# Mixture-of-experts loop: down-projection sums in the gate's banks, an earlier routing plan and an earlier row load

## The reference

```
probs = softmax(ht @ router); vals, idx = top_k(probs, 2)
gates = weights of the two chosen experts, normalised to sum 1
for e in range(8):
    out += gates[:, e:e+1] * (silu(ht @ w_gate[e]) * (ht @ w_up[e])) @ w_down[e]
```

## Time and profile before

| | us |
|---|---|
| median of 3 runs | 1326.36 |
| lowest and highest of them | 1324.71, 1326.44 |
| the profiled execution | 1324.71 |
| its span, first to last instruction | 1322.5 |
| PE busy | 1273.0 |
| DVE busy | 929.1 |
| ACT busy | 820.6 |

### The profile page before, as it was taken

The page is one execution under the profiler, slowest core; times in us unless marked ns, Lnnn a source line. Parts: engine busy times, 40 slices in busy tenths (PEclk is TensorE's granted clock), DMA queues, the critical chain, the costliest instruction groups (busy, mean ns, idle before and its releaser), DMA issues.

```text
span 1322.5 us, 15853 instructions
## 1 busy us (share of the span) xinstructions
PE 1273.0 (96%) x6057; PEld 1034.8 (78%) x6057; DVE 929.1 (70%) x926; ACT 820.6 (62%) x905; POOL 40.8 (3%) x52
## 2 busy tenths in 40 slices
PE   7999999999999899999999999999899998999998
PEld 6888888778887688867886788778678876788886
DVE  4776455446759878899889988998877564645542
ACT  5645444336866677788778877886577565544431
POOL 4001000000000200000000000002010000000000
PEclk9999999999999999999999999999999999999999
DMA  9648654544227989999999999999774241555440
GB/s 324 237 149 271 208 183 168 180 147 133 97 96 294 387 342 372 382 391 396 401 392 389 415 405 380 393 408 394 275 254 160 96 160 64 191 190 191 166 152 32
DMA packets 89855, 339.45 MB, mean 257 GB/s; under 512 B 6267, under 2 KB 14160, under 8 KB 66128
## 3 DMA queue, kind: packets, MB, share of 16 engines
q1 hardware_dynamic: 86816, 328.64, 66.8%
q0 software_dynamic: 2816, 9.89, 2.2%
q10 hardware_dynamic: 160, 0.07, 0.0%
HBM read 332.02 MB, written 9.44 MB: 258 GB/s over the span
## 4 chain that ended last, share of the span: by engine, by line
PE 73%; DVE 10%; issue 6%; ACT 5%; DMA 5%; POOL 0%; SPq 0%; ACTq 0%; DVEq 0%
PE bank L1886 23%; PE bank L1888 22%; PE bank L1887 22%; DVE w_lo L375 7%; DMA raw_beside<-in_moe_w_down 2%; ACT w_hi L370 2%; DMA moe_slots_in<-h,row_to 1%; DMA raw<-in_moe_w_up 1%; PE bank L1998 1%; PE bank L2025 1%; PE bank L2241 1%; DMA raw<-in_conv_w_in 1%; POOL moe_slots_in L592 0%; DMA rows_in<-moe_slots_in 0%; DVE x L1178 0%
## 5 line engine op out<-in xcount | busy, mean ns | idle before, releaser
L375 DVE TENSOR_TENSOR w_lo<-raw,w_hi 128x2048 fp32r<-128x2048 f32 (+3 forms) x246 | 548.4, 2245 | 205.0 <-ACT w_hi L370 204.3
L370 ACT ACTIVATE w_hi<-raw 128x2048 fp32r<-128x2048 f32 (+3 forms) x246 | 460.4, 1882 | 219.6 <-PE bank L1888 200.4
L1886 PE MATMUL bank<-w_hi,xT_hi 128*128 128x512 f32 (+2 forms) x672 | 255.9, 381 | 4.1 <-DVE xT_lo L1150 1.8
L1888 PE MATMUL bank<-w_hi,xT_lo 128*128 128x512 f32 (+2 forms) x672 | 252.9, 376 | 0.0
L1887 PE MATMUL bank<-w_lo,xT_hi 128*128 128x512 f32 (+2 forms) x672 | 252.7, 376 | 0.0
L375 DVE TENSOR_TENSOR w_lo<-raw_beside,w_hi 128x2048 fp32r<-128x2048 f32 x64 | 145.3, 2287 | 14.1 <-ACT w_hi L370 13.7
L1886 PEld LDWEIGHTS bank<-w_hi,xT_hi 128*128 128x128 f32 x672 | 126.4, 188 | 28.4 <-issue 3.6
L370 ACT ACTIVATE w_hi<-raw_beside 128x2048 fp32r<-128x2048 f32 x64 | 122.1, 1919 | 40.3 <-PE bank L1888 26.6
L1888 PEld LDWEIGHTS bank<-w_hi,xT_lo 128*128 128x128 f32 x672 | 126.4, 188 | 22.9
L1887 PEld LDWEIGHTS bank<-w_lo,xT_hi 128*128 128x128 f32 x672 | 126.5, 188 | 21.7
L1886 PE MATMUL bank<-w_hi,gT_hi 128*128 128x512 f32 x320 | 127.7, 399 | 2.1 <-DVE w_lo L375 1.7
(11 more groups left out here) (428 smaller groups left out, 1614.5 us busy)
## 6 DMA issues: line engine op xcount, KB each, us to landing
raw<-in_moe_w_gate SPq DMA_DIRECT2D x48, 1024.0 KB, 6.2
raw<-in_moe_w_up SPq DMA_DIRECT2D x48, 1024.0 KB, 7.9
raw_beside<-in_moe_w_down SPq DMA_DIRECT2D x32, 1024.0 KB, 10.7
raw<-in_moe_w_down SPq DMA_DIRECT2D x32, 1024.0 KB, 11.1
raw<-in_w_gate_up SPq DMA_DIRECT2D x22, 1024.0 KB, 5.2
raw_beside<-in_moe_w_gate SPq DMA_DIRECT2D x16, 1024.0 KB, 5.8
raw_beside<-in_moe_w_up SPq DMA_DIRECT2D x16, 1024.0 KB, 7.1
raw<-in_ffn_w_gate SPq DMA_DIRECT2D x11, 1024.0 KB, 5.1
```

The source lines that it names most:

```text
L370: nc.scalar.activation(w_hi[:, slot, :n], raw_of(i, stream)[:, :n], ACT.Copy).then_inc(stream.high, 1)
L375: nc.vector.tensor_tensor(w_lo[:, slot, :n], raw_of(i, stream)[:, :n], w_hi[:, slot, :n].bitcast(F32), ALU.subtract).then_inc(stream.low, 1)
L1886: mm(dst, a_hi, b_hi, start=start, stop=False)
L1888: return mm(dst, a_lo, b_hi, start=False, stop=stop)
```

## The change

Five things change. The down product of heavy and light experts goes to banks 0 and 1. The next expert's rows are transposed into banks 4 and 5 (heavy) or 6 and 7 (light), and the second folds of a light expert go to banks 4 and 5. PE waits for `moe_y` within the gate, after quarters 2 and 3 of chunks 0 and 1, instead of ahead of up, and asks for both chunks at its start; in `expert_put` it waits ahead of the gate. ACT's wait for `moe_y` ahead of silu and a wait of PE in the light expert go. In position 0 `positions` moves from c = 4 to c = 0, `rows_of_choices` from c = 5 to c = 1, and `load_rows(1)` from behind chunk 20 to behind chunk 14.

```diff
-                        if c == (14 if p else 20) and p < E - 1:
+                        if c == 14 and p < E - 1:
                             load_rows(p + 1)
...
                 def silu(e, number, quarter):
-                    act.wait_ge(sem("moe_y"), 1 + e)
...
-                        ins = A_(M["y"][:, half * HALF:(half + 1) * HALF], bank[4 + half][:, :], ACT.Copy)
+                        ins = A_(M["y"][:, half * HALF:(half + 1) * HALF], bank[half][:, :], ACT.Copy)
...
-                        ins = V.tensor_tensor(M["y"][:LIGHT, cols], bank[4 + half][:LIGHT, :], y_low[:, cols], ALU.add)
+                        ins = V.tensor_tensor(M["y"][:LIGHT, cols], bank[half][:LIGHT, :], y_low[:, cols], ALU.add)
...
-                        if first and c == 4:
+                        if first and c == 0:
                             positions()
-                        if first and c == 5:
+                        if first and c == 1:
                             rows_of_choices()
...
-                def gate(e, product):
-                    for k in range(KD):
+                def gate(e, product, y_read):
+                    first_two = [(k, weights(W1, MOE0 + k, e)) for k in range(2)]
+                    for quarter in (2, 3):
+                        for k, (wh, wl) in first_two:
+                            product(quarter, k, wh, wl, quarter)
+                    pe.wait_ge(sem("moe_y"), y_read)
+                    for k, (wh, wl) in first_two:
+                        for quarter in (0, 1):
+                            ins = product(quarter, k, wh, wl, quarter)
+                        ins.then_inc(W1.used, 1)
+                    for k in range(2, KD):
...
-                    gate(e, light_product)
+                    gate(e, light_product, 1 + e)
                     pe.wait_ge(sem("moe_act_done"), QUARTERS * e)
-                    pe.wait_ge(sem("moe_y"), 1 + e)
...
-                    pe.wait_ge(sem("moe_silu_done"), gated(e, 1))
...
-                        ins = fold_quarter(e_up, 2 + quarter // 2, quarter)
+                        ins = fold_quarter(e_up, 4 + quarter // 2, quarter)
...
-                    turn_rows(bank[0], 0)
-                    turn_rows(bank[1], 1)
+                    turn_rows(bank[4], 0)
+                    turn_rows(bank[5], 1)
...
-                        wide(W1, MOE0 + GU_CHUNKS + c, e, eth, etl, 2 * c, (4, 5), c == 0, c == FE // 256 - 1, tokens=1)
+                        wide(W1, MOE0 + GU_CHUNKS + c, e, eth, etl, 2 * c, (0, 1), c == 0, c == FE // 256 - 1, tokens=1)
...
                 def expert_put(e, h, n, number, job, last):
-                    if not last:
-                        pe.wait_ge(sem("moe_y"), E + 2 * n)
+                    pe.wait_ge(sem("moe_y"), E + 2 * n)
...
-                    if last:
-                        pe.wait_ge(sem("moe_y"), E)
```

More of the change, by code:

```diff
@@ L935, in light @@
                         if c in (17, 18):
-                            rows_high(number + c - 17, c - 17, c - 17)
+                            rows_high(number + c - 17, 6 + c - 17, c - 17)
                     act.wait_ge(W1.used, MOE0 + EXPERT_CHUNKS + EXPERT_CHUNKS * e)
                     for half in range(2):
-                        ins = A_(y_low[:, half * HALF:(half + 1) * HALF], bank[4 + half][LIGHT:, :], ACT.Copy)
+                        ins = A_(y_low[:, half * HALF:(half + 1) * HALF], bank[half][LIGHT:, :], ACT.Copy)
                     ins.then_inc(sem("light_copied"), 1)
@@ L951, in expert @@
                             turn_high(number + 1, 1)
-                            rows_high(number + 2, 0, 0)
+                            rows_high(number + 2, 4, 0)
                         if c == 16:
-                            rows_high(number + 3, 1, 1)
+                            rows_high(number + 3, 5, 1)
                             turn_high(number + 4, 2)
@@ L1578, in light_product @@
                     dve.wait_ge(sem("light_in_psum"), up_turned(i, j))
-                    V.tensor_tensor(M["e_act"][:, j, :], bank[2 + j][:, :], M["e_act"][:, 2 + j, :], ALU.mult)\
+                    V.tensor_tensor(M["e_act"][:, j, :], bank[4 + j][:, :], M["e_act"][:, 2 + j, :], ALU.mult)\
                         .then_inc(sem("moe_act_done"), 1)
@@ L1599, in light @@
                         if c in (17, 18):
-                            rows_low(n_high + c - 17, c - 17, c - 17)
+                            rows_low(n_high + c - 17, 6 + c - 17, c - 17)
                     dve.wait_ge(sem("light_copied"), y_copied(i))
@@ L1623, in expert @@
                             turn_low(n_high + 1, 1)
-                            rows_low(n_high + 2, 0, 0)
+                            rows_low(n_high + 2, 4, 0)
                         if c == 16:
-                            rows_low(n_high + 3, 1, 1)
+                            rows_low(n_high + 3, 5, 1)
                             turn_low(n_high + 4, 2)
@@ L2318, in light @@
                     pe.wait_ge(sem("moe_rows_loaded"), 16 + 16 * e)
-                    turn_rows(bank[0], 0)
-                    turn_rows(bank[1], 1)
+                    turn_rows(bank[6], 0)
+                    turn_rows(bank[7], 1)
                     for c in range(FE // 256):
@@ L2327, in light @@
                                 cols = slice(k * D + half * HALF, k * D + (half + 1) * HALF)
-                                ins = both(bank[4 + half][:, :], eth[:, 2 * c + k, :], wh[:, cols], wl[:, cols],
+                                ins = both(bank[half][:, :], eth[:, 2 * c + k, :], wh[:, cols], wl[:, cols],
                                            c == 0 and k == 0, c == FE // 256 - 1 and k == 1)
@@ L2333, in expert @@
                     pe.wait_ge(sem("moe_drained"), number)
-                    gate(e, product)
+                    gate(e, product, 1 + e)
                     pe.wait_ge(sem("moe_act_done"), QUARTERS * e)
```

## The result

| | before | after |
|---|---|---|
| median of 4 runs, us | 1325.53 | 1339.51 |
| lowest and highest of them | 1320.38, 1326.44 | 1336.96, 1342.08 |
| the profiled execution | 1324.71 | 1337.59 |
| its span | 1322.5 | 1335.4 |

The ratio after to before is 1.0113, with a 95% interval of 1.0081 to 1.0146: slower, as forecast, but by 14 us where +6.1 was forecast, and with 1338 as the upper end of the range.

A forecast was written before the change was run, and what follows sets the result against it. PE, busy 1273.0 of 1322.5 us, was taken as the bound. Terms -3.3 + 5.6 + 3.8 + 0 = +6.1 us on 1324.7 gave 1330.8, or 1332.5 against the median of 1326.36; range 1327.8 to 1338.

The forecast's parts named there:

- Part 1: Position 0, earlier plan and row load: gains 3.3 us; ends nothing and 5.9 us gained.
- lands at 450.0 ... and waits 2.6 us: Position 0: chunk 15, issued at 444.4, lands at 450.0, is ready at 454.1, and PE waits 2.6 us for it.
- the clock stays up: Position 0: with the next rows landed at 450, no waits of 1.50 and 4.34 us, so no lower clock at down.
- slower by SP: Rival: SP's wait for the indirect DMAs delays chunks 15 on, part 1 gains nothing: 1335.8; clock drop adds 1.5. Chance 0.12.
- The share of the indirect DMAs beside the loads: Position 0: by the rows less than a quarter, some 92 of 412 GB/s; half would give the 5.9 us end.
- Part 2: Light to heavy, positions 2 to 3 and 4 to 5: 2.8 us lost at each, 5.6 together.
- 2.2 are the second chunk: Start of positions 3 and 5: of 2.8 us lost, 2.2 wait for chunk 1's split, 0.6 for y's addition.
- The lower clock that I kept as an end: Part 2's upper end, 2 x 4.3 us; as a rival, a slow chunk (+1.5) per boundary: 1335.5, chance 0.18.
- Part 3: Light to last, position 6 to 7: PE waits for moe_y before its first matmul; loses 3.8 us, ends 2.3 and 5.8.
- with a smaller wait behind it I take back 2.0: Position 7: a late PE waits less for the e_act that had cost 1.54 us, so 2.0 us come off the loss.
- Part 4: Remaining edits, including y's copies after a heavy expert and ACT's moe_y wait: cost nothing; cover for y's copies 0.5 us.
- faster: Rival: weight stream bounds the pairs, light experts regain boundary waits, parts 2 and 3 fall to about 0: 1323.1. Chance 0.08.

The follow-up runs named there:

- store_late_load18: Kernel before with position 0's store of y moved from behind chunk 13 to behind 22 and the row load behind chunk 18: 1320.01 us, 0.9967.
- plan_only: Kernel before with the position 0 edits alone (positions at c = 0, rows_of_choices at c = 1, row load behind chunk 14): 1325.33 us, 1.0013.
- before_again: The kernel before, unchanged, run once more for a second profile: 1325.68 us.
- plan_mid: store_late_load18 with positions at c = 2 and rows_of_choices at c = 3: 1317.70 us, 0.9961 against before.
- plan_mid_load14: plan_mid with the row load behind chunk 14, as in the change: 1325.49 us, 1.0014 against before.
- plan0_load18_store_late: plan_mid with the plan at c = 0 and 1 as in the change; row load behind 18, late store of y: 1320.23 us, 0.9966 against before.
- banks_one_by_one: banks_only with a gate that asks for chunk 1 only behind quarters 2 and 3 of chunk 0: 1334.95 us, 1.0095 against before.
- banks_y_first: banks_one_by_one with DVE adding y ahead of its split of the next expert's chunk 2: 1328.40 us, 1.0027 against before.
- banks_only: Kernel after with plan and row load put back to c = 4, c = 5 and chunk 20: 1337.78 us, 1.0115 against before.
- banks_put_busy: banks_one_by_one with 46 small matmuls, results never read, ahead of the wait of position 7: 1332.33 us, 1.0073 against before.
- store_late: Kernel before with position 0's store of y moved from behind chunk 13 to behind chunk 22: 1321.87 us, 0.9976.
- load18: Kernel before with only the row load moved, from behind chunk 20 to behind chunk 18: 1318.67 us, 0.9952.
- load16: Kernel before with only the row load moved, from behind chunk 20 to behind chunk 16: 1324.43 us, 1.0011.

## Why the forecast had the direction and not the size

**Bound.** That PE sets the time held throughout: positions 1, 3 and 5, where no edit touches them, repeat within 0.03 us (70.05 and 70.38; the 68.72 of store_late_load18 comes of its late mark), and each new wait of PE in the heavy experts and the last is found again in their lengths.

**Part 1: forecast -3.3, measured +1.7 (-0.1 to +3.4) as the whole of plan_only.** In after, position 0 is longer by 0.71 us than in before and by 1.47 than in before_again. Right were the first issue at POOL (424.4 forecast, 425.52 seen), the first wait (1.9, 1.83) and that no wait for the rows is left. The step that failed is "lands at 450.0 ... and waits 2.6 us". Chunk 15 was issued 2 us later than I had it (446.40, of which 1.13 is the later start of all), took 7.21 us and not the 5.6 of a short queue in the earlier trace rows, and PE waited 4.65. And "the clock stays up" failed twice. With that, part 1 fell outside its own ends, whose lower was no gain at all. I also left something out: a DVE that plans instead of splitting frees no raw buffer, so the load queue runs thin (248 GB/s for 312), and chunk 14 goes out late on its own. I had followed DVE's delay to PE and not to the loads. It weighs less than SP's stop: with the plan at c = 2 the loads ran thin too (258 GB/s from 424 to 436 us in plan_mid), and PE waited for chunks 14 and 15 only when SP stopped behind 14 (4.78 us in plan_mid_load14).

Which of the two edits took the gain was shown by swapping one at a time: the row load behind 14 costs 5.7 us against behind 18, clock included (plan_mid_load14, plan_mid), the plan at c = 0 costs 1.0 against c = 2 (plan0_load18_store_late, plan_mid), little more than two executions of one kernel differ by. It is the rival "slower by SP", down to its clock drop, though with the boundaries as forecast that rival's time was 1335.8. Its opposite shows where the gain of 3 to 6 us was to be had: the stop of SP did least harm behind 18, and more behind 14 and 16. I read this as a matter of how soon PE needs the chunks that the stop holds back.

The share of the indirect DMAs beside the loads was the other choice in part 1. The Trainium skill ("DMA: Bandwidth & Descriptors", section "Queues, rings and completion order") has each DMA engine take turns between queues, a packet at a time. The 2 MB took from 425.52 to 446.03 in after, some 102 GB/s of the 420 that moved from 436 to 446; equal turns of bytes aren't seen here either, and no run separates the size of the packets from other causes.

**Part 2: forecast 2 x 2.8, measured 5.58 for positions 3 and 5 together** (73.18 + 73.16 - 2 x 70.38, in banks_one_by_one). The sum was exact and its parts were seen, 2.27 and 0.33 us. But "2.2 are the second chunk" was a wrong attribution: with that wait nearly gone the loss stayed. The addition of y ends when it ends, and PE can't be ahead of it by more than the 12 matmuls of the two quarters; so the loss is y's, and at these two boundaries only banks_y_first lowered it. The lower clock that I kept as an end came at one or two boundaries of a trace and not at others: +0.97 us at position 5 of after (74.13 against 73.16), +0.94 at 3 in banks_only. Position 4, which stands ahead of the one and behind the other, was longer in both (61.39 and 61.89 us, where the kernel before had 60.21 and 60.97): PE waited some 1.15 us for a w_lo there, and the granted clock fell to 0.91 and 0.93 from 720 to 730 us. But before_again has 0.83 in that stretch with no new wait ahead of it, and no run kept the clock up there alone, so whether position 4 belongs to the change is open.

**Part 3: forecast 3.8, measured 6.4** (72.56 - 66.16). The wait is 4.25 net, as forecast 4.3, and the clock 2.15 (banks_put_busy) where I had 1.5. The step that failed is "with a smaller wait behind it I take back 2.0". I read the earlier trace rows as a property of position 7; they were a property of one execution. Against that execution the change shows only +4.05 us, which looks like a hit and is not one. For the clock: the Trainium skill ("TensorE: Matmul & The Clock Gate", section "What's actually happening") has activity alone release the throttle, and banks_put_busy agrees, with 1.00 granted instead of 0.56 when 46 small matmuls stood in the wait.

**Part 4: nothing, as forecast.** Position 1 took 70.05 us in both, and the light experts behind positions 1 and 5 took 60.50 and 59.80 us where before they took 61.17 and 59.84.

**The sum.** By the runs: +1.7 for the plan, +5.6 and +6.4 for the boundaries, and about 1 us for each time that the clock falls at positions 3 to 5. That makes 14 to 16, and 15.0 (10.7 to 19.4) is 1.13% of 1325.5. The range ended at 1338 because it left out the sum of all upper ends (0, 8.6 and 5.8, thus 1340.8), and that is about where the kernel came out, though not part by part. The forecast lacks 14.0 - 6.1 = 7.9 us: 5.0 of them are part 1, 2.6 part 3, and what is left is no more than the clock of part 2. The rival "faster" fell: behind the new waits no light expert got shorter by what they cost (positions 4 and 6 of after: +1.18 and -0.04). No rival put the time as high as it came.

What stays open: why store_late gains 3 us, and why the clock falls behind a short wait in one execution and not in the next.

## What to carry to other kernels

Before a wait is moved ahead in an in-order DMA queue, count how long it will stand and when the chunks that it holds back are needed; behind 18 and behind 14 differed by 5.7 us, and one number changed alone (load18) beat both kernels. Where a wait guards the reuse of a buffer, find what the producer of its signal does just before: putting the addition ahead of one split took 2.0 us off positions 3 and 5 and 4.0 off position 7, which rearranging the consumer could not. A stall that one trace shows needs a second trace of the same kernel before anything is taken back against it.

## What the runs showed of the hardware that I had not expected

The indirect DMAs landed sooner where SP sent fewer weight loads beside them. The earlier trace rows are for a row load behind chunk 20; the answers for L592 are, for 18 (load18), for 16 (load16) and for 14 (plan_mid_load14):

```profile
DMA to landing us min/median/max: 11.2/12.6/13.7
```
```profile
DMA to landing us min/median/max: 8.1/9.5/10.1
```
```profile
DMA to landing us min/median/max: 9.0/9.7/10.7
```

The place of the row load alone doesn't set it: in after, also behind 14 but with more loads and the store of y sent while they were issued, they took 9.8/11.6/13.1 us.

The clock does not follow from the length of a wait alone. Behind the same wait at chunk 4, 1.83 us in after and 1.82 in plan_only, it fell in the one and not in the other:

```profile
422.00:430.00 8.00, 6.42 (x21) 5.17 (x22) 7.79 (x17) 3.49 (x2) 4.18 (x2) 0.79 0.59 173
```
```profile
422.00:430.00 8.00, 6.83 (x28) 5.28 (x29) 7.79 (x17) 3.05 (x3) 5.13 (x3) 1.00 0.73 218
```
